# A float32 model block on one core: half of a step table on GpSimd, and query/key projections of the second attention carried as side products of the first

## The chip, the cores and the metric

The kernel runs on one core of a Trainium2 chip. The metric is device time in microseconds (us), lower is better. The kernel before took 3866.5 us, the median of three runs (3866.39 to 3875.27). All arithmetic is float32; a float32 matmul appears in the trace as two TensorE entries.

## The reference, cut to what matters

The model has a first block (two layers), then a second block of two layers, whose second layer is an attention mixer followed by a mixture of experts. Only the mixer is touched. From the normed hidden state `h` (512 tokens, width 1024) it computes:

```python
q_c, k_c, v_c, q_idx, k_idx, w_idx, q_d, k_d, v_d = split_cols_2(h @ w_in, CD_SIZES)
# first attention ("top-k"): 8 heads of 64; each query keeps the 128 keys with the best index score
score = relu(q_idx . k_idx), weighted by w_idx and summed over 8 index heads; causal
logit_c = q_c . k_c / 8 + bias_c[rel_bucket(dist)];  out_c = softmax(logit_c) @ v_c
# second attention ("diff"): 4 heads, two 64-wide halves each
b_d = rel_bias[:, 8:][rel_bucket(dist_d)]
attn = softmax(q1 . k1 / 8 + b_d) - lam * softmax(q2 . k2 / 8 + b_d);  out_d = attn @ v_d
```

`rel_bucket` maps a distance between positions to one of 32 buckets, and `rel_bias` holds one number for each bucket and each of the 12 heads. So a bias table of 12 heads x 512 queries x 512 keys is needed.

## The kernel before, in words

The kernel is a row of stages with a barrier of all engines between them; within a stage every engine runs its own program in a fixed order and waits on semaphores. The stages that matter here follow each other: `attn_front` (line 2267), the top-k attention, the diff attention (both `attention`, line 620), then `norm_and_out` (line 2492).

`attn_front` is one list of TensorE jobs (built in lines 2291 to 2364, run by `phase`, line 282). Each job writes one of eight PSUM banks in turn, and ScalarE moves it to SBUF. There are first the index projections and 32 index scores (line 2305), and six head projections q_c, k_c, v_c, q_d, k_d, v_d with four jobs each (one for 128 tokens: eight matmuls with 512 columns). Four scores follow each of the first six head jobs, and four bias jobs each of the next 16. The list is what sets the order on TensorE.

A bias job makes a part of the bias table. The 128 partitions hold four groups of 32 buckets, one for each quarter of a 128-query tile; `step[b, key] = 1` where the key is at most a bucket edge away from the query (line 2419, VectorE, one instruction with 512 columns for one query in each of the four quarters). The table of bias differences (128 x 48, block diagonal) times a step gives the bias of 12 heads for four queries. One bias job `g` (line 2322) does two steps, side by side in the array with output partitions 0 to 47 and 64 to 111. There are 64 jobs and three step buffers of two steps. ScalarE moves 112 rows to `out` (line 2338), and SyncE stores every second job's pair with two DMAs (line 2390) into a table in DRAM; ScalarE may reuse an `out` buffer when its store has landed.

VectorE, once the scores are summed, finds the best 128 keys: 16 rounds over four tiles, each a MAX8 (line 2449) and a MATCH_REPLACE8 (line 2450), and after each tile one pair of steps (`make_steps`, line 2414), which waits until the bias job that last used its buffer is done. The masks (lines 2455 and 2456) follow. GpSimd does nearly nothing in this stage.

`attention` runs 32 steps (head pair, query tile, head of the pair) of 128 queries x 512 keys. For each step: TensorE scores (line 754, in pairs), VectorE adds bias and finds the maximum (line 884), ScalarE takes the exponential (line 846), VectorE divides (line 903, or 908 for the difference), TensorE turns the probabilities (line 764), ScalarE moves them (line 829), TensorE weighs the values every four steps (line 782), VectorE stores (line 915). Before that queries and keys, which lie with tokens in the partitions, are turned on TensorE (line 741) and moved (lines 820 and 873). SyncE loads the bias from DRAM, and GpSimd adds the mask to it (line 687). With `side` an attention carries eight more projections: each is eight matmuls in its own bank, two after every step (`side_product`, line 718), its weights loaded by SyncE (line 711), its result moved by ScalarE (line 838). The four attentions of the first block do so; the two touched here do not.

Of the kernel before, what the change touches and what calls it, by code (L numbers as in the profile page):

```python
# [28 lines left out]
P = 128  # L29
# [9 lines left out]
HD = 64  # L39
# [580 lines left out]
def attention(chip, name, q, k, v, dk, out, gate=None, causal=True, scale=1.0, bias=None, masks=None, mix=None, decay=None,  # L620
              side=None, cleared_rows=None, scratch=None, early=None):
# [8 lines left out]
    fills = 2 if packed else 4  # L630
    with chip.stage(name) as st:
        n_turned = 2 * (1 if packed else 2)
        if scratch is None:
            turned_sb = [st.sb(f"turned{i}", [P, SEQ]) for i in range(2 * n_turned)]
        else:
            turned_sb = [part(scratch, i * SEQ, SEQ) for i in range(2 * n_turned)]
# [23 lines left out]
        def turned(which, m, a):  # L660

            return turned_sb[(m % 2) * n_turned + 2 * (0 if packed else a) + which]

        if bias is not None:
# [6 lines left out]
            def _(sp):  # L671
                for g in range(units):
# [26 lines left out]

        if side:  # L700
            side_w = [st.sb(f"side_w{i}", [P, DC, P]) for i in range(2)]
            side_loaded = [st.count(f"side_w{i}_loaded") for i in range(2)]
            side_summed, side_moved = st.count("side_summed"), st.count("side_moved")

            @st.block.sync
            def _(sp):
                for n, (w, _) in enumerate(side_jobs):
                    if n >= 2:

                        sp.wait_ge(*side_summed.at(n - 1))  # L710
                    sp.dma_start(side_w[n % 2][:, :, :], w.rearrange("(k p) n -> p k n", p=P)).then_inc(*side_loaded[n % 2].inc(16))
# [5 lines left out]
        def _(pe):  # L717
# [26 lines left out]
            def score(s):  # L744
                m, i, a = place(s)
                if i == 0:
# [65 lines left out]
        def _(act):  # L812
# [46 lines left out]
            for n in range(n_side):  # L859
                act.activation(side_jobs[n][1], side_jobs[n][1], ACT.Sigmoid)  # L860
# [1406 lines left out]
def attn_front(chip, io, fm, mod, scratch, topk, diff, causal, masks, ex, lambda_init):  # L2267
# [3 lines left out]
    Q4, M, N_SCORES, PAIRS = P // 4, 4 * BIAS_HEADS, TILES * IDX_HEADS, P // 2  # L2271
    STEPS, OUTS = 3, 2
    nq, nk = IDX_HEADS * IDX_DIM, IDX_DIM
    with chip.stage("attn_front") as st:
# [4 lines left out]
        steps_ = [st.sb(f"step{i}", [P, 2, SEQ]) for i in range(STEPS)]  # L2279
# [3 lines left out]
        cleared, pos_landed, table_landed = st.count("table_cleared"), st.count("positions_landed"), st.count("table_landed")  # L2283
# [75 lines left out]
        for n, job in enumerate(heads.jobs):  # L2359
# [3 lines left out]
            elif n < 22:  # L2363
                add_biases(4)
# [940 lines left out]
```

## Time and profile before

| | us |
|---|---|
| median of three runs | 3866.5 |
| the profiled execution | 3888.67 |
| its span in the profile | 3887.0 |
| TensorE busy in the span | 3343.7 (86%) |
| VectorE busy | 1586.1 (41%) |
| ScalarE busy | 722.0 (19%) |
| GpSimd busy | 194.9 (5%) |

The profile is of one execution. Its chain of waits that ended last reaches back only over the final stage, since the barriers cut it; so each stage is read by itself. In the views PE is TensorE, PEld its weight loads, DVE VectorE, ACT ScalarE, POOL GpSimd, SP SyncE; L12 is line 12 of the kernel. A matmul's end is modelled, so the time from one start to the next says more than its duration. PEclk is the granted TensorE clock as a share of full speed.

### The profile page before, as it was taken

The page shows a single profiled execution, that of the slowest core. Times are in us where ns is not written, and L with a number is a line of the kernel's source. Part 1 is how long each engine was busy: PE and PEld are TensorE (multiplying, and loading weights), DVE is VectorE, ACT ScalarE, POOL GpSimd, SP SyncE. Part 2 cuts the span into 40 slices and gives each one's busy share as a digit, 9 for nine tenths or more (in the row PEclk, how much of TensorE's full clock was granted, in tenths as well). Part 3 has the DMA queues.
Part 4 walks back from the last instruction along what each step waited for, and adds up shares of the span by engine and source line. Part 5 has one row for each costly group of instructions (what it writes and reads, how often), then busy time and mean ns, then how long its engine had stood idle before and what let it go on. Part 6 is the DMA issues. An engine that isn't in the chain of part 4 may idle for free. (4 is left out here: it accounts for less than half of the span.)

```text
span 3887.0 us, 42458 instructions
## 1 busy us (share of the span) xinstructions
PE 3343.7 (86%) x16176; PEld 1594.3 (41%) x16177; DVE 1586.1 (41%) x3043; ACT 722.0 (19%) x1428; POOL 194.9 (5%) x263
## 2 busy tenths in 40 slices
PE   8998997999899999799989767779599878688775
PEld 4454442774445443377334422223243344323221
DVE  3335556564314555766456400000248775100002
ACT  2132304111113321311001100000132353000001
POOL 0001010001000001000100000000100230000000
PEclk9999998999999999899999889999799999799997
DMA  2214461104211245100522589999433421999996
GB/s 95 83 38 172 149 215 41 29 8 149 96 44 49 65 141 160 32 20 7 197 87 83 237 368 428 428 428 361 131 118 120 102 66 53 385 427 423 429 428 276
DMA packets 208103, 696.55 MB, mean 179 GB/s; under 512 B 22248, under 2 KB 105704, under 8 KB 182736
## 3 DMA queue, kind: packets, MB, share of 16 engines
q1 hardware_dynamic: 178576, 589.42, 39.7%
q0 software_dynamic: 29376, 105.05, 7.4%
q8 instruction: 102, 1.67, 0.2%
q14 instruction: 49, 0.40, 0.0%
HBM read 636.14 MB, written 58.28 MB: 179 GB/s over the span
## 5 line engine op out<-in xcount | busy, mean ns | idle before, releaser
L348 PE MATMUL bank<-fm,w 128*128 128x512 f32 (+1 forms) x912 | 398.9, 598 | 14.2 <-DMA w<-in_ab_w_in 7.8
L2849 PE MATMUL bank<-experts_wu,experts_hs 128*64 128x512 f32 x1120 | 280.0, 658 | 73.6 <-DMA experts_wu<-in_moe_w_up 73.6
L348 PE MATMUL bank<-w,fm 128*128 128x512 f32 (+2 forms) x768 | 314.7, 566 | 6.2 <-DMA w<-in_w_in 6.2
L2849 PE MATMUL bank<-experts_wg,experts_hs 128*64 128x512 f32 x1120 | 267.4, 633 | 54.0 <-DMA experts_wg<-in_moe_w_gate 44.5
L2914 DVE TENSOR_TENSOR fm<-bank,fm 128x512 f32<-128x512 f32 x35 | 37.0, 1056 | 668.1 <-PE bank L2849 668.1
L2849 PE MATMUL bank<-experts_wd,fm 128*64 128x512 f32 x1120 | 254.8, 608 | 45.1 <-issue 22.9
L348 PEld LDWEIGHTS bank<-fm,w 128*128 128x128 f32 (+1 forms) x912 | 172.8, 190 | 237.7 <-issue 221.9
L729 PE MATMUL bank<-fm,side_w 128*128 128x512 f32 x512 | 249.4, 612 | 6.7 <-DMA side_w<-in_w_in 5.3
L348 PEld LDWEIGHTS bank<-w,fm 128*128 128x128 f32 x768 | 141.9, 195 | 178.5 <-issue 153.4
L2849 PEld LDWEIGHTS bank<-experts_wu,experts_hs 128*64 128x64 f32 x1120 | 86.4, 151 | 265.2 <-issue 170.5
L2849 PEld LDWEIGHTS bank<-experts_wg,experts_hs 128*64 128x64 f32 x1120 | 93.7, 145 | 223.8 <-issue 220.5
L2921 DVE TENSOR_TENSOR fm<-bank,mod 128x512 f32<-128x512 f32 x70 | 45.1, 686 | 326.4 <-PE bank L2849 326.4
L2849 PEld LDWEIGHTS bank<-experts_wd,fm 128*64 128x64 f32 x1120 | 82.9, 139 | 194.5 <-issue 166.0
L846 ACT ACTIVATE prob<-bank,nmax 128x128 f32<-128x128 f32 (+2 forms) x192 | 111.3, 580 | 210.8 <-DVE nmax L894 145.4
L729 PEld LDWEIGHTS bank<-fm,side_w 128*128 128x128 f32 x512 | 90.6, 196 | 88.8 <-issue 82.1
L2893 ACT ACTIVATE fm<-bank 128x512 f32<-128x512 f32 x35 | 20.9, 597 | 554.1 <-PE bank L2849 554.1
L1997 DVE SCALAR_TENSOR_TENSOR ada_sums<-ada_w,cond,ada_sums 128x1024 f32<-128x1024 f32 x84 | 105.8, 1282 | 37.4 <-DMA ada_w<-in_ada_w 36.5
L348 PE MATMUL bank<-w,merged 128*128 128x512 f32 x256 | 113.1, 600 | 3.1 <-DVE merged L1443 3.1
L2889 ACT ACTIVATE experts_hs<-bank 128x512 f32<-128x512 f32 x70 | 38.0, 595 | 409.1 <-PE bank L2841 409.1
L348 PE MATMUL bank<-o_fm,w 128*128 128x512 f32 x240 | 106.7, 604 | 6.5 <-DMA w<-in_w_pc 6.5
L764 PE MATMUL bank<-consts,prob 128*128 128x128 f32 x512 | 78.8, 282 | 29.1 <-ACT pT L829 11.5
L430 PE MATMUL bank<-fm,w 128*128 128x512 f32 x224 | 102.1, 610 | 1.6 <-ACT rwkv_a L1364 1.6
(492 smaller groups left out, 4618.6 us busy)
## 6 DMA issues: line engine op xcount, KB each, us to landing
experts_wg<-in_moe_w_gate SPq DMA_DIRECT2D x64, 2048.0 KB, 19.5
experts_wu<-in_moe_w_up SPq DMA_DIRECT2D x64, 2048.0 KB, 18.8
experts_wd<-in_moe_w_down SPq DMA_DIRECT2D x64, 2048.0 KB, 19.6
ada_w<-in_ada_w POOLq DMA_DIRECT2D x96, 512.0 KB, 4.9
expert_rows<-fm POOLq DMA_DIRECT2D x35, 512.0 KB, 10.4
fm<-expert_rows SPq DMA_DIRECT2D x33, 512.0 KB, 21.6
w<-in_w_in SPq DMA_DIRECT2D x16, 1024.0 KB, 5.5
side_w<-in_w_in SPq DMA_DIRECT2D x32, 512.0 KB, 4.0
```

Of the source, the lines that this page charges most:

```text
L348: ins = pe.matmul(bank, lhsT, rhs, start=(n == 0), stop=(n == len(todo) - 1))
L430: last = pe.matmul(out, lhsT, rhs, start=(n == 0), stop=(n == len(pairs) - 1))
L729: last = pe.matmul(SIDE[:, :], side_w[n % 2][:, k_, :], side_h[:, k_, :], start=(k_ == 0), stop=(k_ == DC - 1))
L764: last = pe.transpose(T[n % 2][:, j * P:(j + 1) * P], prob[s % 4][:, j * P:(j + 1) * P], chip.ident)
L846: act.activation(prob[s % 4][:, 0:n], S[s % n_scores][:, 0:n], ACT.Exp, bias=nmax[:, s:s + 1], scale=1.0 if bias is None else -1.0, accum_ ...
L1997: ins = dve.scalar_tensor_tensor(sums, self.slot[n % self.slots][:, :], by, sums, ALU.mult, ALU.add)
L2849: ins = pe.matmul(bank[rows, :], lhs[:, k, rows], weights[:, s, k, cols], start=(k == 0), stop=(k == chunks - 1))
L2889: ins = act.activation(hs[:, 4 * n:4 * n + 4, :], B[6 + n][:, :].rearrange("p (k n) -> p k n", k=4), ACT.Copy)
L2893: act.activation(act_out[:, :], B[0][:, :], ACT.Silu).then_inc(*silued.inc())
L2914: dve.tensor_tensor(dealt(hid[:, :], FC), B[1][:, :].rearrange("p (q k) -> p q k", k=FC), act_out[:, :].rearrange("p (q k) -> p q k", k=FC ...
L2921: ins = dve.tensor_tensor(y[:, cols], B[4 + d][:, :], gate_row[:, cols], ALU.mult)
```

## The change

Two things are changed.

First, the bias table. Steps are made in fours: VectorE makes two of each four, GpSimd the other two with the same instruction and a semaphore of its own. There are two buffers of four steps in place of three of two. A four has two bias jobs, one for each half of the partitions: job `half` takes 64 partitions of the four steps and of the table, and its four matmuls (64 partitions, 24 rows out) go to four column groups of the array, the other half's to the other 64 rows of the array and another bank. A four is stored by four DMAs in place of two. Seven bias jobs follow each head job from the seventh on, in place of four. VectorE makes its steps after every second tile in place of every tile.

Second, q_d and k_d (eight of the 24 head jobs) leave `attn_front`. The top-k attention carries them as eight side products, weights times `fm`, so that they come out with the head width in the partitions, as the diff attention wants them; the scale goes into ScalarE's move. The top-k attention then has three score banks in place of four. The diff attention gets them already turned, and does without its turning and its moves. Side weights are loaded by SyncE after the bias of the same number. The turned buffers of the top-k attention lie in the second half of `y`.

```diff
-    fills = 2 if packed else 4
+    fills = 0 if turned_in else 2 if packed else 4
...
-        if scratch is None:
+        if turned_in:
+            turned_sb = []
...
-            turned_sb = [part(scratch, i * SEQ, SEQ) for i in range(2 * n_turned)]
+            turned_sb = [part(scratch, scratch_at + i * SEQ, SEQ) for i in range(2 * n_turned)]
...
+            if turned_in:
+                return (q, k)[which][:, m, :]
...
+            def load_side(sp, n):
+                if n >= 2:
+
+                    sp.wait_ge(*side_summed.at(n - 1))
+                sp.dma_start(side_w[n % 2][:, :, :], side_jobs[n][0].rearrange("(k p) n -> p k n", p=P)
+                             ).then_inc(*side_loaded[n % 2].inc(16))
...
+                    if g < n_side:
+                        load_side(sp, g)
...
-                if i == 0:
+                if i == 0 and not turned_in:
...
-                    act.activation(side_jobs[n][1], SIDE[:, :], ACT.Copy).then_inc(*side_moved.inc())
+                    act.activation(side_jobs[n][1], SIDE[:, :], ACT.Copy, scale=side_scales[n] if side_scales else 1.0
+                                   ).then_inc(*side_moved.inc())
...
+    STEPS, OUTS = 2, 2
...
+        steps_ = [st.sb(f"step{i}", [P, 4, SEQ]) for i in range(STEPS)]
...
-        def bias(g):
-
-            b = g // 2
+        def bias(j):
+
+            f, half = divmod(j, 2)
+            rows, cols = slice(2 * Q4 * half, 2 * Q4 * (half + 1)), slice(TWO * half, TWO * (half + 1))
 
             def first(pe, moved):
-                pe.wait_ge(*stepped.at(g + 1))
+                if half == 0:
+                    pe.wait_ge(*stepped.at(f + 1))
+                    pe.wait_ge(*stepped_too.at(f + 1))
 
             def pairs(pe, bank):
-                for a in range(2):
-                    ins = pe.matmul(bank[64 * a:64 * a + M, :], table[:, :], steps_[g % STEPS][:, a, :], start=True, stop=True,
-                                    tile_position=(0, 64 * a))
+                for a in range(4):
+                    ins = pe.matmul(bank[Q4 * a:Q4 * a + TWO, :], table[rows, cols], steps_[f % STEPS][rows, a, :], start=True, stop=True,
+                                    tile_position=(2 * Q4 * half, Q4 * a))
                 return ins
 
             def ahead(act, moved):
-                if g % 2 == 0 and b >= OUTS:
-                    act.wait_ge(*stored[b % OUTS].at(32 * (b // OUTS)))
+                if half == 0 and f >= OUTS:
+                    act.wait_ge(*stored[f % OUTS].at(4 * 16 * (f // OUTS)))
             return Job(None, pairs, lambda bank: bank[:, :], "act", lambda act, ps: act.activation(
-                outs[b % OUTS][0:64 + M, g % 2, :], ps[0:64 + M, :], ACT.Copy), first, ahead)
+                outs[f % OUTS][0:P - Q4 + TWO, half, :], ps[0:P - Q4 + TWO, :], ACT.Copy), first, ahead)
...
-        for names, dsts in ((("q_c", "k_c", "v_c"), topk), (("q_d", "k_d", "v_d"), diff)):
+        for names, dsts in ((("q_c", "k_c", "v_c"), topk), (("v_d",), (diff_v,))):
...
             if n < 6:
                 add_scores(4)
-            elif n < 22:
-                add_biases(4)
-        dst = scratch.rearrange("a t n k -> a (t n) k")
+            else:
+                add_biases(min(7, 2 * FOURS - len(biased_at)))
+        dst = scratch.rearrange("(q r) t n k -> r q (t n) k", q=2)
...
-            while 2 * begun[0] + 1 < PAIRS and biased_at[2 * begun[0] + 1] < upto:
-                b = begun[0]
-                sp.wait_ge(*moved(biased_at[2 * b + 1]))
-                for a in range(2):
-                    sp.dma_start(dst[:, 4 * b + a:4 * b + 4:2, :], outs[b % OUTS][64 * a:64 * a + M, :, :]).then_inc(*stored[b % OUTS].inc(16))
+            while begun[0] < FOURS and biased_at[2 * begun[0] + 1] < upto:
+                f = begun[0]
+                sp.wait_ge(*moved(biased_at[2 * f + 1]))
+                for a in range(4):
+                    sp.dma_start(dst[:, :, 4 * f + a, :], outs[f % OUTS][Q4 * a:Q4 * a + TWO, :, :]).then_inc(*stored[f % OUTS].inc(16))
                 begun[0] += 1
...
+            pool.wait_ge(*quartered.at(1))
+            for f in range(FOURS):
+                if f >= STEPS:
+                    pool.wait_ge(*done(biased_at[2 * (f - STEPS) + 1]))
+                for a in (2, 3):
+                    at = at_quarter + 4 * f + a
+                    ins = pool.tensor_scalar(steps_[f % STEPS][:, a, :], pos[:, 0:SEQ], pos[:, at:at + 1], None, ALU.is_le)
+                ins.then_inc(*stepped_too.inc())
...
-            def make_steps(g):
-                if g >= STEPS:
-                    dve.wait_ge(*done(biased_at[g - STEPS]))
+            def make_steps(f):
+                if f >= STEPS:
+                    dve.wait_ge(*done(biased_at[2 * (f - STEPS) + 1]))
                 for a in range(2):
-                    at = at_quarter + 2 * g + a
-                    ins = dve.tensor_scalar(steps_[g % STEPS][:, a, :], pos[:, 0:SEQ], pos[:, at:at + 1], None, ALU.is_le)
+                    at = at_quarter + 4 * f + a
+                    ins = dve.tensor_scalar(steps_[f % STEPS][:, a, :], pos[:, 0:SEQ], pos[:, at:at + 1], None, ALU.is_le)
                 ins.then_inc(*stepped.inc())
...
-                        g += 1
+                    if t % 2 and f < FOURS:
+                        make_steps(f)
+                        f += 1
...
                 attention(chip, "topk_attention", q, k, lambda h, j: v[:, j, h, :], HD, y_fm, causal=False,
-                          scale=HD ** -0.5, bias=bias_of, masks=masks)
+                          scale=HD ** -0.5, bias=bias_of, masks=masks,
+                          side=(fm, [(io["cd_w_in"][0][:, CD[name] + c * P:CD[name] + (c + 1) * P], dst[:, c, :])
+                                     for name, dst in (("q_d", diff_q), ("k_d", diff_k)) for c in range(DIFF_HEADS)]),
+                          scratch=y_fm, scratch_at=DIFF_HEADS * SEQ, side_scales=[HD ** -0.5] * DIFF_HEADS + [1.0] * DIFF_HEADS)
...
-            attention(chip, "diff_attention", q, k, lambda m, j: vd[:, j, m, :], HD, mixed, causal=False, scale=HD ** -0.5,
+            vd = diff_v[:, :, :, :].rearrange("p t (h a) d -> p t h (a d)", a=2)
+            attention(chip, "diff_attention", diff_q, diff_k, lambda m, j: vd[:, j, m, :], HD, mixed, causal=False, turned_in=True,
```

## Rows read from the trace of the kernel before

**Rows 1.** Stretches: bounds, width, busy PE, PEld, DVE, ACT, POOL, then PEclk, DMA share, GB/s.
```profile
3070.60:3152.10 81.50, 61.06 (x352) 32.51 (x352) 58.03 (x140) 42.36 (x100) 38.57 (x16) 0.92 0.43 104
...
3152.10:3223.00 70.90, 52.33 (x224) 28.52 (x224) 58.94 (x156) 34.78 (x84) 18.90 (x8) 0.95 0.23 60
2886.50:3056.60 170.10, 170.10 (x513) 62.83 (x512) 141.94 (x317) 47.79 (x80) 0.00 (x0) 1.00 0.36 111
```

**Rows 2.** Timeline, TensorE in attn_front: start, us, engine, line, operation, operands, count.
```profile
2954.30 3.64 PE L2331 MATMUL bank<-step,table 128*48 128x512 f32 x16
2957.87 7.13 PE L348 MATMUL bank<-w,fm 128*128 128x512 f32 x16
...
3053.59 14.00 PE L348 MATMUL bank<-w,fm 128*128 128x512 f32 x32
```

**Rows 3.** Timeline, VectorE in attn_front; in brackets the idle time before, with its releaser.
```profile
2887.42 0.69 DVE L2449 MAX8 best<-attn_masks 128x8 f32<-128x512 f32 x1
...
2955.84 0.88 DVE L2419 TENSOR_SCALAR step<-pos 128x512 f32<-128x512 f32 x2 [1.78 <-PE bank L2331]
2956.64 0.69 DVE L2449 MAX8 best<-attn_masks 128x8 f32<-128x512 f32 x1
...
3053.51 0.69 DVE L2449 MAX8 best<-attn_masks 128x8 f32<-128x512 f32 x1
...
3056.55 0.43 DVE L2455 TENSOR_SCALAR attn_masks<-attn_masks 128x512 f32<-128x512 f32 x1
...
3060.57 0.69 DVE L2456 TENSOR_TENSOR attn_masks<-attn_masks,attn_causal 128x512 f32<-128x512 f32 x1
```

**Rows 4.** Two pairs of score matmuls on different row halves of the array, timeline.
```profile
3110.97 1.13 PE L754 MATMUL bank<-turned 64*128 64x512 f32 x4
```

**Rows 5.** GpSimd's groups of instructions: busy us, mean ns, then idle time before.
```profile
L687 POOL TENSOR_TENSOR bias<-bias,attn_masks 128x1024 f32<-128x1024 f32 x16 | 38.6, 2425 | 297.0 <-DMA bias<-bias_scratch 296.9
...
L694 POOL MEMSET zero<- 128x1024 f32 x1 | 1.0, 951 | 356.4 <-POOLq L120 356.4
```

**Rows 6.** Timeline of the top-k attention: VectorE's division beside GpSimd's mask additions, and alone.
```profile
3107.71 4.83 POOL L687 TENSOR_TENSOR bias<-bias,attn_masks 128x1024 f32<-128x1024 f32 x2 [0.62 <-DMA bias<-bias_scratch]
...
3108.09 2.24 DVE L903 TENSOR_SCALAR prob<-prob,sums 128x512 f32<-128x512 f32 x1
...
3113.88 0.49 DVE L903 TENSOR_SCALAR prob<-prob,sums 128x512 f32<-128x512 f32 x1
```

**Rows 7.** Lines 2338 and 2390: count, ns min/median/max, first and last start; landing time.
```profile
L2338 ACT ACTIVATE out<-bank x64: 597/597/600, 2891.6 to 3053.7; 112x512 f32<-112x512 f32 x64
...
L2390 SPq DMA_DIRECT2D bias_scratch<-out x64: 302/384/687, 2893.1 to 3054.7; - x64
...
DMA to landing us min/median/max: 2.4/2.8/6.5
```

**Rows 8.** Timeline, TensorE in the top-k attention around a long wait.
```profile
3092.87 1.12 PE L764 MATMUL bank<-consts,prob 128*128 128x128 f32 x4 [2.48 <-DVE prob L903]
3093.91 2.08 PE L754 MATMUL bank<-turned 64*128 64x512 f32 x4
```

**Rows 9.** Timeline, TensorE in an attention of the first block that carries eight side products.
```profile
1316.16 0.63 PE L741 MATMUL bank<-consts,fox_q 128*128 128x128 f32 x4 [1.05 <-PEq L120]
...
1321.07 5.30 PE L729 MATMUL bank<-fm,side_w 128*128 128x512 f32 x8
...
1414.12 1.74 PE L782 MATMUL bank<-pT,fox_v 128*64 128x256 f32 x16 [0.69 <-ACT pT L829]
```

**Rows 10.** Timeline, SyncE at the start of the top-k attention: bias loads.
```profile
3070.69 11.11 SPq L678 DMA_DIRECT2D bias<-bias_scratch  x24
```

**Rows 11.** DMA issues on the page: out<-in, engine, count, KB each, us to landing.
```profile
side_w<-in_w_in SPq DMA_DIRECT2D x32, 512.0 KB, 4.0
```

**Rows 12.** VectorE's moves of turned keys in the diff attention: busy us, mean ns.
```profile
L873 DVE COPY turned<-bank 128x512 f32<-128x512 f32 x4 | 2.7, 683 | 2.3 <-PE bank L741 2.3
```

More of the change, by code:

```diff
@@ L620, in attention @@
 def attention(chip, name, q, k, v, dk, out, gate=None, causal=True, scale=1.0, bias=None, masks=None, mix=None, decay=None,
-              side=None, cleared_rows=None, scratch=None, early=None):
+              side=None, side_scales=None, turned_in=False, cleared_rows=None, scratch=None, scratch_at=0, early=None):
     steps, pairs = HEADS * TILES, HEADS // 2
@@ L660, in turned, with _ @@
         def turned(which, m, a):
+            if turned_in:
+                return (q, k)[which][:, m, :]
             return turned_sb[(m % 2) * n_turned + 2 * (0 if packed else a) + which]
+        if side:
+            side_w = [st.sb(f"side_w{i}", [P, DC, P]) for i in range(2)]
+            side_loaded = [st.count(f"side_w{i}_loaded") for i in range(2)]
+            side_summed, side_moved = st.count("side_summed"), st.count("side_moved")
+            def load_side(sp, n):
[3 more added lines that the diff above has]
+                             ).then_inc(*side_loaded[n % 2].inc(16))
+            if bias is None:
+                @st.block.sync
+                def _(sp):
+                    for n in range(n_side):
+                        load_side(sp, n)
         if bias is not None:
@@ L698, in _ @@
                 pool.wait_ge(*wiped.at(wiped.total))
[L700 to L711, printed above, removed]
         if early is not None:
@@ L858, in _ @@
                 act.wait_ge(*side_moved.at(n_side))
-            for n in range(n_side):
+            for n in range(n_side if side_scales is None else 0):
                 act.activation(side_jobs[n][1], side_jobs[n][1], ACT.Sigmoid)
@@ L2264, in conv_mixers, with attn_front @@
         routed.programs()
-def attn_front(chip, io, fm, mod, scratch, topk, diff, causal, masks, ex, lambda_init):
+def attn_front(chip, io, fm, mod, scratch, topk, diff_v, causal, masks, ex, lambda_init):
     w_in = io["cd_w_in"][0]
-    Q4, M, N_SCORES, PAIRS = P // 4, 4 * BIAS_HEADS, TILES * IDX_HEADS, P // 2
-    STEPS, OUTS = 3, 2
+    Q4, N_SCORES, M = P // 4, TILES * IDX_HEADS, 4 * BIAS_HEADS
+    FOURS, TWO = P // 4, 2 * BIAS_HEADS
+    STEPS, OUTS = 2, 2
     nq, nk = IDX_HEADS * IDX_DIM, IDX_DIM
@@ L2278, in attn_front @@
         lam, pr = st.sb("lam", [P, 4, HD]), st.sb("pr", [P, 2, HD])
-        steps_ = [st.sb(f"step{i}", [P, 2, SEQ]) for i in range(STEPS)]
+        steps_ = [st.sb(f"step{i}", [P, 4, SEQ]) for i in range(STEPS)]
         outs = [st.sb(f"out{i}", [P, 2, SEQ]) for i in range(OUTS)]
@@ L2432, in _ @@
             link(dve.tensor_tensor(table[:, :], table[:, :], before[:, :], ALU.subtract))
-            for g in range(STEPS):
-                make_steps(g)
+            for f in range(STEPS):
+                make_steps(f)
             for n in range(N_SCORES):
@@ L2444, in _ @@
                 dve.wait_ge(*added.at(n + 1))
-            g = STEPS
+            f = STEPS
             for _ in range(TOPK // 8):
@@ L2473, in attn_mixers @@
         with ExitStack() as diff_heads:
-            diff = [sb(f"diff_{n}", [P, TILES, 2 * DIFF_HEADS, HD], diff_heads, side="right") for n in "qkv"]
+            diff_q, diff_k = (sb(f"diff_{n}", [P, DIFF_HEADS, SEQ], diff_heads, side="right") for n in "qk")
+            diff_v = sb("diff_v", [P, TILES, 2 * DIFF_HEADS, HD], diff_heads, side="right")
             with ExitStack() as topk_heads:
                 topk = [sb(f"topk_{n}", [P, TILES, HEADS, HD], topk_heads, side="right") for n in "qkv"]
-                attn_front(chip, io, fm, mod, scratch, topk, diff, causal, masks, ex, lambda_init)
+                attn_front(chip, io, fm, mod, scratch, topk, diff_v, causal, masks, ex, lambda_init)
                 y_fm = sb("y", [P, DC, SEQ])
```

10 lines of the change are left out of this document (5 added, 5 removed).

## The prediction, made before the changed kernel was run

> **What bounds the kernel now.** The chain that ended last covers only the last stage, so I read the touched stages one by one: first the stretches table, then each engine's timeline inside a stage, then the waits. In attn_front TensorE is busy 170.1 of 170.1 us while VectorE is at 141.9 [rows 1], and VectorE's steps wait for it [rows 3]: TensorE sets the end, VectorE is 16% behind. In the top-k attention (3070.6 to 3152.1, 81.5 us) TensorE is busy 61.1 and VectorE 58.0; in the diff attention (70.9 us) VectorE 58.9 and TensorE 52.3 [rows 1]. So the change takes TensorE work from a stage where it is the bound and puts it where some 20 us of TensorE are idle. What matters is who is next in the first and how far the second grows.
>
> **The front without eight head jobs.** A head job takes 14.0/2 = 7.0 us (3.64 of bias behind it start to start 7.1); I use 7.06, so 8 x 7.06 = 56.5 us leave TensorE [rows 2]. Four bias jobs take 2957.87 - 2954.30 = 3.57 us, 0.89 each, with two column groups side by side [rows 2]. A four is eight matmuls on two row halves and four column groups. Two score pairs on different row halves run together: four entries in 1.13 us, some 0.54 for each of two passes [rows 4]. Eight at once appears nowhere. Bounds for a four are 1.07 (all together, as in [rows 4]) and 2 x 0.89 = 1.79 (halves one after the other); I take 1.07, since both kinds of sharing show. From the start of the seventh head job TensorE then has 10 x 7.06 + 32 x 1.07 = 105 us, where it had 184.
>
> **VectorE is next.** Two tiles of the search without steps take 3056.55 - 3053.51 = 3.04 us, and two steps 2956.64 - 2955.84 = 0.80 [rows 3]. The search has 32 such pairs of tiles, and 30 fours are made within it: 32 x 3.04 + 30 x 0.80 = 121.3 us from 2887.42, so 3008.7; the masks, 3056.55 to 3061.3, add 4.7 [rows 3]. Nothing can end the stage before 3013.4: of the 56.5 + 23 us taken from TensorE at most 55 can come back.
>
> **GpSimd's steps.** No such instruction is in the trace. Lower bound: half a memset of 1024 columns, 0.48 us; upper: half of a two-input addition of 1024 columns, whose mean is 2.43, so 1.21 [rows 5]. One input lies between; I take 0.9, 1.8 a four, under VectorE's 3.84. The price that counts is another: a VectorE division that takes 0.49 us alone took 2.24 beside GpSimd's addition and ended just after its end [rows 6]. The Trainium skill (SBUF — State Buffer, SBUF: two separate sides) says that the pair of ports is locked for a whole instruction and the loser blocks; by that rule moving a step from VectorE to GpSimd can cost VectorE a wait as long as the step, which speaks against this change. What saves it is time: GpSimd starts four f+2 when TensorE is done with f, 1.1 us after VectorE made f, and is through at 2.9, while VectorE is in its 3.04 of search. They meet only when both waited for the same buffer; there I charge 1.0 us. The Trainium skill (GPSIMD Engine Reference, 3.1 Elementwise — side-by-side cycle accounting) has 769 ns for 512 elements in its best case; that would take 0.3 off two such waits and leave the sum.
>
> **The cycle, by hand.** Seven fours go with two head jobs. Let H be the start of a head job, with the last four just half done. VectorE makes the next four at H+3.3, comes to the one after at H+6.4 and waits: its buffer is the half-done one. TensorE ends the head job at 7.1, the half at 8.0, and VectorE, with GpSimd in its way, is done at 9.8 (GpSimd at 10.2). The next is made at 13.6, TensorE done 14.7, second head job to 21.8; meanwhile fours are made at 17.5 and 21.3, then 25.2 and 29.0, and at H+29.9 it starts over. That is 3.0 more than 7 x 3.84. TensorE idles 2.5 to 2.8 us at a time in it. The trace shows what such a wait does: after 2.48 us idle the four turns took 1.12 us and the two score pairs behind them 2.08 [rows 8] for 1.13 [rows 4], the granted clock being at its lower level, 1.2 GHz for 2.4. At half speed for some 3.4 us a head job takes 1.7 more; the one before the blocked buffer passes it on. Period 31.6 us with this, 29.9 without.
>
> The first group has two fours ready; the search waits at 2890.5, and the next head job starts at about 2898.3. Four periods later, at 3024.7 (3017.9 without the clock), all but half a four is done. Then come the last head job 7.06 (+1.7), the last half four 0.9, ScalarE's move 0.6, four stores at 0.38 and a landing of 2.8 [rows 7], 0.5 of barrier: 3039.8, or 3031.3. I take 3037: 33.6, say 34 us earlier than 3070.6. ScalarE and SyncE keep up: two moves, four issues and a landing are 5.5 us, less than the 7.7 in which an out buffer comes round. SyncE's wait for stores holds only the v_d weights back, which have four groups of slack.
>
> **The top-k attention with side products.** An attention of the first block has the same arrangement: eight side products, two matmuls a step, three score banks. It ran from 1316.16 to 1415.86, 99.7 us [rows 9], with causal widths, 5/8 of these on average. Of the 61.1 us here [rows 1] some 5 are turns of q and k and a few the lower clock, so 3/8 of about 50, 19 us, is the most that full widths add; with the fixed part of each matmul 16 (13 to 19). There the first side product starts 4.9 us after the stage [rows 9]; here its weights are issued behind eight bias loads at 0.46 us each [rows 10] and take 4.0 to land [rows 11], so 8.3: +3.4, with nothing behind it on TensorE going ahead, as it works in order. Sum 99.7 + 16 + 3.4 = 119.1, which is +37.6. The other way: 61.1 + 56.5 = 117.6, plus 5 of start and less 3 of clock, 119.6. VectorE's 58 and ScalarE's 42 + 5 us are well under it, and the contention of [rows 6] is now hidden. The side weights wait on SyncE for a side product two before; the bias behind them has eight steps of slack.
>
> **The diff attention.** Its start is set by bias, mask and first maximum, so the early turns save nothing. Of four moves three lie in the body where VectorE is the bound: 3 x 0.68 [rows 12] = 2 us. Between 0 and 4.
>
> **Sum.** -34 + 37.5 - 2 = +1.5 us, on 3888.7 profiled. The profiled execution is 22 us above the median of 3866.5; the difference is put on the median: 3868.
>
> **Rivals.** (1) Faster. The clock stays up in the front's waits (3031.3, -39.3), the widths add 13 and the side weights come in the shadow of the turns (+31.7), diff -4: -11.6, with cheap GpSimd steps -14: 3853. For it: TensorE is in a head job half of the time. Against: waits of 2.5 us. (2) The two row halves do not overlap, so a four takes 1.79. Three fours in a period see it, about 2.5 us, x4, and the tail: +11, 3879. Against it stands [rows 4]. (3) Slower, one mechanism: the GpSimd step. From 1.92 us each (2 x 1.92 = 3.84) GpSimd sets the pace and VectorE meets its lock every time. At 2.43, as much as the addition of twice the columns, VectorE waits some 2.4 us in each of 30 fours, 72 less the 12 it loses now anyway: 60 on top of the sum, 3928. (4) The move does nothing for VectorE: lock waits as long as the saved steps in every four, +0.9 x 30 less 12 = +15: 3883; it needs GpSimd to fall in step with VectorE. The rule of the Trainium skill (SBUF — State Buffer, SBUF: two separate sides) is this rival if the two always meet; [rows 6] bears out the lock, not the meeting.
>
> **How the numbers follow.** Forecast 0.49 (own range 3857 to 3879), rival 1 0.27, rival 2 0.12, rival 3 0.04, rival 4 0.08. Range 3849 to 3886: it leaves out rival 3 and the ends of 1 and 4. About 0.3%, 11.6 us, is what a measurement here tells from no change. Faster 0.28, same 0.48, slower 0.24: rivals 2, 3 and 4 are slower, the forecast counts as same.
>
> **What would show it.** Right: VectorE's search without gaps but one a pair of head jobs, its steps 0.4 to 0.5 us but after those gaps; eight L2331 entries starting within 0.1 us; attn_front 34 us shorter, TensorE under 75% in it; the top-k attention at 119 with TensorE over 93%; the diff attention's start unchanged. Wrong: step instructions on VectorE of over 1 us throughout (rival 4), GpSimd busy without a break (3), a four of 1.8 us (2), granted clock 1.00 in the front (1). A top-k attention under 112 or over 125 us would break the term it rests on most.

## The result, and the profile after

The changed kernel takes 3904.9 us (median of 4 runs, 3900.8 to 3910.7), the kernel before, beside it, 3870.9 (3866.4 to 3877.7): a ratio of 1.0086 [1.0066, 1.0107], 33 us more (26 to 41). I had predicted 3868 with a range up to 3886. The time is 19 us above the end of the range, and slower than before.

The profiled execution of the changed kernel has 3905.1 us and a span of 3903.4. The profiled one of the kernel before has 3888.7, 18 us above its own median, so the two profiles differ by 16 us only; they are compared here stage by stage. First the stretches that answer to [rows 1]: attn_front from the first maximum of the search, the top-k attention, the diff attention. Columns: bounds, width, busy PE, PEld, DVE, ACT, POOL (instructions), granted clock, DMA share, GB/s.

```profile
2875.80:3054.40 178.60, 132.28 (x664) 41.91 (x662) 132.76 (x263) 41.77 (x76) 100.56 (x60) 0.78 0.30 83
3054.40:3173.80 119.40, 113.23 (x480) 54.96 (x480) 54.31 (x140) 47.43 (x108) 37.90 (x16) 0.94 0.45 106
3173.80:3245.00 71.20, 52.02 (x192) 28.80 (x192) 55.84 (x152) 32.68 (x80) 18.86 (x8) 0.86 0.22 60
```

The same three stretches of the kernel before are 183.2, 81.5 and 70.9 us (the first is cut here from the first maximum, 2887.4, to the stage's end, 3070.6; its row):

```profile
2887.40:3070.60 183.20, 180.19 (x536) 67.00 (x534) 145.82 (x324) 50.47 (x84) 0.00 (x0) 1.00 0.34 104
```

So the front is 4.6 us shorter where I had 34, the top-k attention 37.9 longer where I had 37.6, and the diff attention unchanged where I had 2 less. The three together are 33.6 us longer, as much as the medians differ. All other stages, which are the same code, are 17 us shorter in this profile than in the one of before. (11.6 of these lie ahead of the first maximum, and the front's first conversion of positions comes as much earlier.)

The front is where the account failed. Before, TensorE was busy all the time at clock 1.00. Now it is busy 132 of 179 us at 0.78, VectorE 133, GpSimd 101: none of the three is full. That is the sign of a cycle in which they wait for one another. TensorE's timeline shows it (start, us, engine, line, operation; in brackets the idle time before it and its releaser), beside [rows 2]:

```profile
2936.16 1.91 PE L2348 MATMUL bank<-step,table 64*24 64x512 f32 x24
2940.87 1.28 PE L2348 MATMUL bank<-step,table 64*24 64x512 f32 x16 [2.79 <-POOL step L2427]
2944.33 1.95 PE L2348 MATMUL bank<-step,table 64*24 64x512 f32 x16 [2.18 <-POOL step L2427]
2946.21 8.23 PE L348 MATMUL bank<-w,fm 128*128 128x512 f32 x16
2954.38 1.94 PE L2348 MATMUL bank<-step,table 64*24 64x512 f32 x32
2959.18 1.95 PE L2348 MATMUL bank<-step,table 64*24 64x512 f32 x16 [2.86 <-POOL step L2427]
2962.64 1.92 PE L2348 MATMUL bank<-step,table 64*24 64x512 f32 x8 [1.51 <-POOL step L2427]
```

Three things stand in it. A four is sixteen entries (eight matmuls, two passes). Two fours with all data at hand take 1.94 us (the x32 group), 0.97 each: the row halves do overlap. TensorE idles 1.5 to 2.9 us again and again, and here always for a step of GpSimd. And the head job behind such waits takes 8.23, the next one from 2964.48 9.33, for 7.13 before: every head job of the front runs partly at the lower clock. From 2908.52 to 2946.21, seven fours and two head jobs, it is 37.7 us; the mean period is 37.6. I had 31.6.

VectorE's side of the same period, to be read against [rows 3], and GpSimd's:

```profile
2937.36 1.23 DVE L2444 TENSOR_SCALAR step<-pos 128x512 f32<-128x512 f32 x2 [6.71 <-PE bank L2348]
...
2941.53 1.23 DVE L2444 TENSOR_SCALAR step<-pos 128x512 f32<-128x512 f32 x2
...
2955.66 1.23 DVE L2444 TENSOR_SCALAR step<-pos 128x512 f32<-128x512 f32 x2 [1.49 <-PE bank L2348]
```

```profile
2937.34 13.25 POOL L2427 TENSOR_SCALAR step<-pos 128x512 f32<-128x512 f32 x8 [9.14 <-PE bank L2348]
2955.65 10.18 POOL L2427 TENSOR_SCALAR step<-pos 128x512 f32<-128x512 f32 x6 [5.06 <-PE bank L2348]
```

VectorE's pair of steps takes 1.23 us or more nearly every time, not only behind a wait: GpSimd, once released, works 13 us without a break and so nearly always runs beside it (56 of VectorE's 64 steps). The pace of VectorE without waits is 2941.53 - 2937.36 = 4.17 us a four where I had 3.84. And once in a period it waits 6.7 us for the buffer of a four whose second half TensorE does only behind the head job.

The price of a GpSimd step is the number that the trace of before did not have (count, ns min/median/max, first and last start). In the stretch ahead of the search, with VectorE idle but for its first moments, and then in the search:

```profile
L2427 POOL TENSOR_SCALAR step<-pos x4: 1550/1553/1658, 2797.5 to 2802.2; 128x512 f32<-128x512 f32 x4
```

```profile
L2427 POOL TENSOR_SCALAR step<-pos x60: 1554/1720/1844, 2880.2 to 3035.9; 128x512 f32<-128x512 f32 x60
```

1.55 us alone, where my bounds were 0.48 and 1.21. The 1.72 is the median of two kinds: 25 of the 64 steps, with VectorE idle or in its search, have a median of 1.56, and the 39 that overlap a step of VectorE 1.78. One of each, and the pair of VectorE's steps that meets the second:

```profile
2939.17 1.56 POOL L2427 TENSOR_SCALAR step<-pos 128x512 f32<-128x512 f32 x1
2940.70 1.78 POOL L2427 TENSOR_SCALAR step<-pos 128x512 f32<-128x512 f32 x1
2941.53 0.49 DVE L2444 TENSOR_SCALAR step<-pos 128x512 f32<-128x512 f32 x1
2941.93 0.83 DVE L2444 TENSOR_SCALAR step<-pos 128x512 f32<-128x512 f32 x1
```

VectorE's first step begins and ends, at its usual 0.49 us, while GpSimd's step from 2940.70 to 2942.48 is still running; only the second is longer, by 0.34. The two slow each other when their steps meet, but neither keeps the other out for a whole step.

The waits of the whole front (engine and line, what it waited for: us in total, times, longest):

```profile
PE bank L2348 <- POOL step L2427: 41.8, 18, 2.9
DVE step L2444 <- PE bank L2348: 34.2, 9, 6.8
```

The 41.8 and 34.2 us lie partly beside each other, so they are not a sum. Which of the causes (the price, the shared port, the blocked buffer, the clock) carries how much, the trace does not say; the experiments do.

### The profile page after: what moved, and what is told of

Read it like the earlier page. It is cut to its first block and busy times, and to the rows that moved or that the text cites. A ratio compares the mean times of both kernels' runs of the same rounds, so it can differ in the third digit from the quotient of the medians.

```text
span 3903.4 us, 42897 instructions
## 1 busy us (share of the span) xinstructions
PE 3351.6 (86%) x16400; PEld 1588.3 (41%) x16401; DVE 1564.8 (40%) x2975; ACT 715.9 (18%) x1424; POOL 301.3 (8%) x327
## 5 line engine op out<-in xcount | busy, mean ns | idle before, releaser
L348 PE MATMUL bank<-fm,w 128*128 128x512 f32 (+1 forms) x912 | 399.5, 599 | 12.7 <-DMA w<-in_ab_w_in 7.6
L740 PE MATMUL bank<-fm,side_w 128*128 128x512 f32 x640 | 314.3, 616 | 8.5 <-DMA side_w<-in_w_in 5.5
L348 PE MATMUL bank<-w,fm 128*128 128x512 f32 (+2 forms) x640 | 273.0, 585 | 6.3 <-DMA w<-in_w_in 6.3
L348 PEld LDWEIGHTS bank<-w,fm 128*128 128x128 f32 x640 | 123.7, 205 | 162.6 <-issue 150.6
L740 PEld LDWEIGHTS bank<-fm,side_w 128*128 128x128 f32 x640 | 113.7, 197 | 116.8 <-issue 107.8
L2427 POOL TENSOR_SCALAR step<-pos 128x512 f32<-128x512 f32 x64 | 106.8, 1684 | 146.6 <-PE bank L2348 133.3
```

Of the source, the lines that this page charges most:

```text
L348: ins = pe.matmul(bank, lhsT, rhs, start=(n == 0), stop=(n == len(todo) - 1))
L740: last = pe.matmul(SIDE[:, :], side_w[n % 2][:, k_, :], side_h[:, k_, :], start=(k_ == 0), stop=(k_ == DC - 1))
L2427: ins = pool.tensor_scalar(steps_[f % STEPS][:, a, :], pos[:, 0:SEQ], pos[:, at:at + 1], None, ALU.is_le)
```

## The experiments

The theory before the first four was that the two halves of the change each do what their stages show, and that GpSimd's price sets the front. In the table, "front" is from the first maximum to the end of attn_front (the first bias load of the next stage), "period" seven fours with two head jobs, all from the profiles; the ratio is against the kernel before on the same chip.

| kernel | ratio [95%] | front us | period us | head jobs us |
|---|---|---|---|---|
| before | 1 | 183.2 | | 7.1 |
| after | 1.0086 [1.0066, 1.0107] | 178.6 | 37.6 | 8.2 to 9.5 |
| side_only | 1.0059 [1.0034, 1.0084] | 170.5 | | 7.1 to 9.3 |
| table_gpsimd_only | 0.9923 [0.9902, 0.9945] | 156.1 | | 7.1 |
| table_vector_only | 0.9921 [0.9898, 0.9944] | 158.3 | | 7.1 |
| all_steps_on_vector | 1.0073 [1.0048, 1.0098] | 175.9 | 37.3 | 8.1 to 9.6 |
| whole_fours | 1.0017 [0.9999, 1.0034] | 146.8 | 30.7 | 7.1, 7.7 |
| whole_fours_vector | 1.0023 [1.0010, 1.0035] | 153.4 | 32.4 | 7.1 to 9.1 |
| half_steps | 1.0043 [1.0025, 1.0061] | 161.4 | 34.2 | 8.8 to 9.3 |
| half_columns | 1.0029 [1.0016, 1.0042] | 162.2 | 34.3 | 8.7 to 9.1 |
| four_buffers | 0.9975 [0.9956, 0.9995] | 137.0 | 29.4 | 7.1 to 9.4 |
| four_buffers_whole | 0.9978 [0.9965, 0.9992] | 136.9 | 29.4 | 7.1 to 9.2 |

**side_only**: the bias table of before, with the side products of the change.

```diff
-                for a in range(4):
-                    ins = pe.matmul(bank[Q4 * a:Q4 * a + TWO, :], table[rows, cols], steps_[f % STEPS][rows, a, :], start=True, stop=True,
-                                    tile_position=(2 * Q4 * half, Q4 * a))
+                for a in range(2):
+                    ins = pe.matmul(bank[64 * a:64 * a + M, :], table[:, :], steps_[g % STEPS][:, a, :], start=True, stop=True,
+                                    tile_position=(0, 64 * a))
```

> The bias table stays as in the kernel before (pairs of steps, three buffers, VectorE alone, two column groups); only the query and key projections of the diff attention move to side products, and the 64 bias jobs are dealt seven to each of the last ten head jobs. Theory A (the front is paced by whoever makes the steps, and GpSimd's 1.7 us step is what took the gain): VectorE needs 64 x 1.52 + 61 x 0.80 + 4.7 = 151 us from its first MAX8, plus some 5 of waits and a tail of 13 (head job, last bias, store), so the front ends about 20 us earlier than before; the top-k attention 119 us (+38): total +17 us. Rival B (the side products cost 38 us and the front cannot give anything back whatever makes the steps): +34 us, as with the whole change.

It is 23 us slower (13 to 33), between the two expectations. The front is 12.7 us shorter, the top-k attention 118.6 us. Moving eight head jobs out of the front buys 13 us there and costs 37 in the attention.

**table_gpsimd_only** and **table_vector_only**: the change's table without the side products, once with GpSimd's half and once with all four steps on VectorE.

```diff
-        for names, dsts in ((("q_c", "k_c", "v_c"), topk), (("v_d",), (diff_v,))):
+        for names, dsts in ((("q_c", "k_c", "v_c"), topk), (("q_d", "k_d", "v_d"), diff)):
-                add_biases(min(7, 2 * FOURS - len(biased_at)))
+                add_biases(min(4, 2 * FOURS - len(biased_at)))
```

and table_vector_only besides, with GpSimd's loop left out:

```diff
-                for a in range(2):
+                for a in range(4):
```

> Only the bias table is changed (fours, two row halves, half of the steps on GpSimd); the projections stay in the front as 24 head jobs, and four bias jobs follow each head job from the seventh on. Theory A: two fours a head job need 2 x 3.44 = 6.9 us of GpSimd, which fit into the 7.1 us of the head job and 2.0 us of bias; TensorE keeps the front with 16 x 9.2 + 14.1 us and it ends some 20 us earlier than before; both attentions as before: total -20 us. Rival B (GpSimd's steps and the port lock cost wherever they stand): the front no shorter than before, total 0 to +15 us.

> As the run with the bias table alone, but VectorE makes all four steps of each four (no GpSimd). Theory A: VectorE's 32 x 3.04 + 30 x 1.60 + 4.7 = 150 us fit under TensorE's 161, so this too ends the front some 20 us earlier: total -20 us, within 5 us of the run with GpSimd. Rival B: 15 us or more faster than the run with GpSimd.

Both are 30 us faster than before, the best of all kernels here; I had expected 20. The front of the first:

```profile
2934.95 1.94 PE L2348 MATMUL bank<-step,table 64*24 64x512 f32 x32
2936.82 7.13 PE L348 MATMUL bank<-w,fm 128*128 128x512 f32 x16
2943.88 1.94 PE L2348 MATMUL bank<-step,table 64*24 64x512 f32 x32
2945.75 7.13 PE L348 MATMUL bank<-w,fm 128*128 128x512 f32 x16
```

TensorE never waits, the clock stays up, and the bias behind a head job costs 1.87 us start to start (2945.75 - 2943.88) where 3.57 stood in [rows 2]. GpSimd's step costs 1.72 us here as well, and it does not matter:

```profile
L2427 POOL TENSOR_SCALAR step<-pos x64: 1552/1722/1847, 2789.8 to 3003.9; 128x512 f32<-128x512 f32 x64
```

As long as TensorE is the bound, neither GpSimd's price nor who makes the steps shows in the ratios. (The front of the second is 2.2 us longer: from 2952.58 on its head jobs start every 9.24 us for 8.94, which is two of VectorE's 4.6 us a four with four steps in each.) The two halves of the change alone give -30 and +23, and together +33, not -7: some 40 us are lost by their meeting (each of the three is known to 8 or 10 us).

**all_steps_on_vector**: the whole change, but GpSimd makes nothing.

```diff
-            pool.wait_ge(*quartered.at(1))
-            for f in range(FOURS):
...
-                ins.then_inc(*stepped_too.inc())
...
-                for a in range(2):
+                for a in range(4):
```

> The whole change, but VectorE makes all four steps. Theory A: the blocked four costs 1.6 us of VectorE in place of 3.4 of GpSimd, the period of seven fours falls from 37.6 to about 34.9 us, the front is 12 us shorter than with the whole change: +22 us against before. Rival B (not GpSimd but the two buffers, the seven bias jobs in a row and the clock set the front): no shorter than with the whole change, +34 us or more, since VectorE has 24 us more to do.

This fell out against the theory that GpSimd's price sets the front: the front is 2.7 us shorter than the changed kernel's, not 12, with GpSimd away altogether. The ratio, +28 us (19 to 38), lies between the two expectations and does not decide. VectorE now makes four steps in 1.67 us, and waits once a period:

```profile
2963.49 1.67 DVE L2435 TENSOR_SCALAR step<-pos 128x512 f32<-128x512 f32 x4
...
2973.05 1.67 DVE L2435 TENSOR_SCALAR step<-pos 128x512 f32<-128x512 f32 x4 [4.98 <-PE bank L2347]
2977.66 1.67 DVE L2435 TENSOR_SCALAR step<-pos 128x512 f32<-128x512 f32 x4
```

Its pace is 4.61, and 7 x 4.61 + 4.98 = 37.3 is the period. So the second theory: seven bias jobs behind a head job are three fours and a half. The half-done four keeps one of the two step buffers through a whole head job, whoever makes the steps. The runs that follow test this from several sides.

**whole_fours** and **whole_fours_vector**: eight and six bias jobs by turns, so that no four is split.

```diff
-                add_biases(min(7, 2 * FOURS - len(biased_at)))
+                add_biases(min(6 if n % 2 else 8, 2 * FOURS - len(biased_at)))
```

> After, with eight and six bias jobs by turns behind the head jobs instead of seven each, so that no four is half done when a head job runs. Theory A (a half-done four holds one of the two step buffers through a whole head job, and the waits that this makes are the 8 us a period that are missing): seven fours and two head jobs take 29.5 to 32 us instead of 37.6, the front is some 20 to 30 us shorter than the changed kernel's 178.6, and the whole 4 to 14 us longer than before. Theory B (GpSimd's 1.72 us a step and the port that it shares with VectorE set the front, however the jobs are grouped): the period stays above 36 us, the front within 6 us of 178.6, the whole 28 to 36 us longer than before.

> All steps on VectorE, none on GpSimd, and eight and six bias jobs by turns. Theory A (the blocked buffer): the one wait of 4.98 us that all_steps_on_vector had in each period goes, the period is VectorE's own 4.61 x 7 = 32.3 us instead of 37.3, the front some 20 us shorter than that kernel's 175.9, and the whole 6 to 14 us longer than before. Theory B (the grouping is beside the point): front within 5 us of 175.9, the whole 22 to 34 us longer than before.

Both came as the blocked buffer has it: fronts 31.8 and 22.5 us shorter than with sevens, periods 30.7 and 32.4. The waits of whole_fours:

```profile
DVE step L2444 <- PE bank L2348: 6.5, 9, 1.4
...
PE bank L2348 <- POOL step L2427: 33.3, 14, 2.9
```

VectorE's waits fall from 34.2 to 6.5 us, though TensorE still waits 33 for GpSimd, and the head jobs are back at 7.1 and 7.7:

```profile
2925.54 1.09 PE L2348 MATMUL bank<-step,table 64*24 64x512 f32 x16 [2.87 <-POOL step L2427]
2926.55 7.13 PE L348 MATMUL bank<-w,fm 128*128 128x512 f32 x16
```

The grouping alone is worth some 27 us (1.0086 against 1.0017). Between these two, GpSimd's half is worth 6.6 us of front; the ratios do not part them.

**half_steps** and **half_columns** take GpSimd's price away and leave the sevens. In the first GpSimd makes nothing and TensorE reads VectorE's two steps twice (half of the queries get a wrong bias); in the second GpSimd writes 256 of its 512 columns (half of the keys in half of the queries).

```diff
-                    ins = pe.matmul(bank[Q4 * a:Q4 * a + TWO, :], table[rows, cols], steps_[f % STEPS][rows, a, :], start=True, stop=True,
+                    ins = pe.matmul(bank[Q4 * a:Q4 * a + TWO, :], table[rows, cols], steps_[f % STEPS][rows, a % 2, :], start=True, stop=True,
```

```diff
-                    ins = pool.tensor_scalar(steps_[f % STEPS][:, a, :], pos[:, 0:SEQ], pos[:, at:at + 1], None, ALU.is_le)
+                    ins = pool.tensor_scalar(steps_[f % STEPS][:, a, 0:SEQ // 2], pos[:, 0:SEQ // 2], pos[:, at:at + 1], None, ALU.is_le)
```

> After without GpSimd's half of the steps: VectorE makes the first two of each four and TensorE reads them in the place of the other two as well, so the bias table is wrong for half of the queries. The grouping in sevens stays. It is the changed kernel with GpSimd's steps at no price and no shared port: VectorE's pace falls to 3.04 + 0.80 = 3.84 us a four, which is what the prediction reckoned with. Theory A (the blocked buffer alone makes the waits): one wait a period stays, 3.84 x 7 + 5 to 8 = 32 to 35 us, and the front is 13 to 25 us shorter than 178.6; the whole 9 to 21 us longer than before. Theory B (GpSimd's price made the waits): the period is 28.5 to 31 us, as the prediction had it, the front 28 to 36 us shorter, and the whole within 8 us of before.

> After with GpSimd writing only the first 256 of the 512 columns of each of its steps; the other 256 are zeroed once, so half of the bias table is wrong. Sevens and two buffers stay. Theory A (GpSimd's price is by the column and by VectorE's use of the port): a step takes 0.78 to 0.95 us, which is the 0.9 that the prediction took, a pair of VectorE's steps 1.0 to 1.25 us, the period 34.5 to 36.5 us, between the 34.2 of half_steps and the 37.6 of the changed kernel, and the front 163 to 173 us; the whole 17 to 28 us longer than before. Theory B (a fixed price for each instruction of GpSimd): a step stays above 1.3 us, and the period at 37 to 38 us. If the front falls to 150 us or less, the account of the clock is wrong.

```profile
L2429 POOL TENSOR_SCALAR step<-pos x64: 910/921/1284, 2796.6 to 3021.3; 128x256 f32<-128x256 f32 x64
```

half_columns happens to give a step the very price that I had put in, 0.92 us, so it is close to the kernel that my sum described. Its period is 34.3 (a hair under what I expected of it) and not 31.6, with every head job slowed:

```profile
2904.15 1.95 PE L2348 MATMUL bank<-step,table 64*24 64x512 f32 x16 [1.92 <-DVE step L2446]
2906.02 8.83 PE L348 MATMUL bank<-w,fm 128*128 128x512 f32 x16
2914.79 1.94 PE L2348 MATMUL bank<-step,table 64*24 64x512 f32 x32
2918.39 1.09 PE L2348 MATMUL bank<-step,table 64*24 64x512 f32 x16 [1.66 <-POOL step L2429]
2921.39 1.92 PE L2348 MATMUL bank<-step,table 64*24 64x512 f32 x8 [1.92 <-DVE step L2446]
2923.24 8.76 PE L348 MATMUL bank<-w,fm 128*128 128x512 f32 x16
```

The whole is 11 us longer than before (6 to 16), less than the 17 to 28 that I had expected of it, though the three stages in its profile are 17 us longer (352.8 for 335.6). half_steps, 17 us longer than before as expected (10 to 24), has VectorE at my 3.84 a four and its one long wait, beside one of 1.9 in each period:

```profile
2919.73 0.88 DVE L2435 TENSOR_SCALAR step<-pos 128x512 f32<-128x512 f32 x2 [5.62 <-PE bank L2347]
...
2923.56 0.88 DVE L2435 TENSOR_SCALAR step<-pos 128x512 f32<-128x512 f32 x2
...
2927.38 0.88 DVE L2435 TENSOR_SCALAR step<-pos 128x512 f32<-128x512 f32 x2
```

GpSimd for nothing, or at 0.92 us a step, is the same front (161.4, 162.2). So a price of 0.9 is indeed hidden; one of 1.72 is not: 178.6 - 162.2 = 16.4 us.

**four_buffers** and **four_buffers_whole**: the third and fourth step buffer lie in diff_q and diff_k, which the top-k attention fills only later; the second has the eight and six by turns too.

```diff
-    STEPS, OUTS = 2, 2
+    STEPS, OUTS = 4, 2
-        steps_ = [st.sb(f"step{i}", [P, 4, SEQ]) for i in range(STEPS)]
+        steps_ = [st.sb(f"step{i}", [P, 4, SEQ]) for i in range(2)] + [diff_q, diff_k]
```

> After with four step buffers instead of two (the third and fourth lie in the memory of the turned queries and keys of the second attention, which is free until the front is over); sevens stay and GpSimd still makes half. Theory A (too few buffers for a head job of 7 to 9 us): VectorE's waits for TensorE go, VectorE paces the loop at 4.18 us a four with two fours more made ahead, 32 x 3.04 + 28 x 1.23 = 132 us from the first maximum to the end of the loop, the front 147 to 155 us instead of 178.6, and the whole from 2 us less to 10 us more than before. Theory B (GpSimd's steps at 3.44 us a four are late whenever TensorE asks): TensorE still waits for GpSimd, the front 165 to 178 us, the whole 20 us or more longer than before.

> Four step buffers and eight and six bias jobs by turns, together. Theory A (four_buffers already leaves VectorE with next to no waits, so VectorE's own 132 us are the floor of the loop): the front is within 4 us of the 137.0 of four_buffers, and the whole 4 to 14 us less than before. Theory B (each cure takes its own part of the 42 us): the front is 128 us or less, the whole 18 us or more less than before.

137.0 us of front, and VectorE is at last the bound (130.5 busy of 137.0):

```profile
2879.30:3016.30 137.00, 111.96 (x664) 39.09 (x662) 130.48 (x258) 41.89 (x76) 92.20 (x56) 0.89 0.39 108
```

It is 10 us less than the least that I had expected: the search ends after 131.4 us (at 3010.7), as reckoned with 132, but then TensorE has nothing left to catch up with, and the stage ends 5.6 us later and not 15. The grouping adds nothing to it (136.9): with four buffers a half-done four blocks nobody, and 137 is VectorE's floor. That is the change made as well as I know how, and it is 10 us faster than before (2 to 17), against 30 for the table alone. The reason can be read off the fronts. The table alone ends at 156.1, and VectorE's floor is 137: taking eight head jobs away buys at most 19 us, and the top-k attention grows by 37 for it.

## Why the prediction was wrong, step by step

- **"TensorE sets the end, VectorE is 16% behind", "VectorE is next"**: right. With four buffers the front ends at VectorE's own work.
- **A four at 1.07 us**: right; 1.09 alone (half of one alone takes 1.06), 1.94 for two in a row. Rival 2 is out.
- **"The top-k attention 119.1"**: right, 119.4 with TensorE busy 95%. Its first side product starts 3063.13 - 3054.44 = 8.7 us into the stage (8.3 said), 3.8 later than in the stage that I had built on; that leaves 119.4 - 99.7 - 3.8 = 15.9 for the wider rows, where I had 16. So both terms are right, each for itself:

```profile
3063.13 4.64 PE L740 MATMUL bank<-fm,side_w 128*128 128x512 f32 x5 [1.68 <-DMA side_w<-in_cd_w_in]
```

- **"GpSimd's steps ... I take 0.9"**: the step that failed first. 1.55 us alone, 1.72 in the median of the front. The upper bound was half of a two-input addition of 1024 columns, 1.21 [rows 5]; I had reasoned that one input must be cheaper than two. By the undisturbed steps of half_columns a column costs (1550 - 910)/256 = 2.5 ns and an instruction 0.27 us on top. So half of an instruction is no bound for an instruction of half the width: the part on top does not halve. If it is the same for the addition, which no run shows, 512 columns of it would take 0.27 + (2.43 - 0.27)/2 = 1.35 us (an estimate), and the comparison against a column of scalars is dearer than that too. The Trainium skill (GPSIMD Engine Reference, 3.1 Elementwise — side-by-side cycle accounting) gives 769 ns for 512 elements at best, the nearest figure to one input; the trace has twice that. The price of the steps is worth 16.4 us of the 29 missing (178.6 against half_columns' 162.2).
- **"They meet only when both waited for the same buffer; there I charge 1.0 us"**: wrong in how often. GpSimd at 3.44 us a four has no gap before VectorE's next pair; the pair takes 1.23 instead of 0.88 us in nearly every four, 0.35 x 7 = 2.4 us a period. The Trainium skill (SBUF — State Buffer, SBUF: two separate sides) has an exclusive hold for a whole instruction. The trace does not agree for these steps: one of VectorE's runs from 2941.53 to 2942.02 at its usual 0.49 us in the middle of one of GpSimd's (2940.70 to 2942.48), 26 of the 64 lie wholly inside one, and the wait "as long as the step" never came; it was 0.35 us a pair, a fifth of GpSimd's step. This was what rival 4 had (VectorE pays in every four) at some 40% of its price, 0.35 for 0.9, and rival 3's condition (1.92 us) nearly met: it took both. I had given them 0.12 together and priced each as if the other did not happen.
- **"At half speed for some 3.4 us a head job takes 1.7 more", on one of two head jobs**: right on the mechanism and on the size (8.7 to 9.1 us in half_columns for 7.1), wrong on the count. In half_columns both head jobs of a period are slowed, and the bias jobs before each take 1.95 us for 1.09. The second head job alone adds 1.7 and the bias jobs 1.7 more, part of it beside waits that were there anyway: 34.3 us a period for my 31.6. The clock is not all of these 2.7 us: VectorE comes to the blocked buffer 4.8 us after the head job's start (3.8 in the changed kernel), not 6.4, and waits there for 5.1. How much of it is the clock's and how much that of the hand cycle's order, no run shows. The front of half_columns is 162.2 where my sum has 183.2 - 34 = 149.2: 13 us. Four periods make 11 of it. 3 more come from my own rounding: the hand cycle ended at 3039.8 and I took 3037, without a reason; some 1 us goes the other way. 13 + 16.4 = 29 is what is missing from -34.
- **The hand cycle** had the half-done four and VectorE's wait for it, and gave 31.6 us. What I did not do was ask what the cycle would be without it. With whole fours 31.8 us of front go, both terms above together: they are not prices that must be paid but what the blocked buffer makes of them, since VectorE's 4.18 us a four are more than GpSimd's 3.44. (A slip beside it: from 3070.6 to 3013.4, the least end that I had worked out, are 57 us and not 55; nothing hangs on it.)
- **The diff attention, -2**: all four moves are gone (VectorE has 152 instructions for 156, and is busy 55.8 us for 58.9 [rows 1]) and the stage is as long as before. From its start to the first maximum are 7.2 us in both, as I said. The saved work turned into idle time; the granted clock there is 0.86 for 0.95 before, and whether that took the gain was not tried.
- **Chances**: slower by over 0.3% had 0.24. The profile had what was needed to give it more: a sum of +1.5 made of -34 and +37.5, of which the second was bounded closely by a stage of the same kind, and the first rested on a price that no row showed and a cycle of three engines with two buffers. In that cycle a clock that stayed up gave 6 us (3037 to 3031.3), while every price that I had too low made a wait in each period. The range should have reached further up than down; it was laid evenly round the sum.

## What to carry to other kernels

When work is taken from the bound of a stage, look first at how far the next engine is below it: here 19 us were to be had for 37 paid, and that alone decided against the move. When two or three engines hand buffers round, count the buffers against the longest job that can come between two halves of one hand-over; a group size that is no multiple of the unit cost 27 us, and two more buffers in memory that was free took that cost away. A price that the trace does not show is safely bounded only by the same operation at the same width; the bound from half of another one failed here.

## What the runs showed of the chip

- GpSimd's comparison of 512 columns with a column of scalars takes 1.55 us alone and 1.56 beside VectorE's search, and 1.78 where it overlaps VectorE's steps; of 256 columns 0.92. VectorE does 512 in 0.49.
- Beside it, two such steps of VectorE take 1.23 us for 0.88. A whole one of them, 0.49 us, can run while GpSimd's is under way.
- Eight matmuls of 64 rows by 24 columns, on two row halves and four column groups, take 1.09 us together and 0.97 in a row of them; the four of one row half alone take 1.06.
- Waits of 1.5 to 2.9 us between short jobs can put the granted clock to its lower level (1.2 GHz for 2.4) for the job behind them: 8.2 to 9.5 us in the changed kernel for head jobs of 7.1. They need not: with one wait of 2.87 us in whole_fours the head job takes 7.1, with one of 2.74 in half_steps 9.2. Waits of 0.9 to 1.2 us, three ahead of each head job, did not in side_only once the job had run at 7.1 (its first ones took 7.7 to 9.3):

```profile
2966.31 1.07 PE L2343 MATMUL bank<-step,table 128*48 128x512 f32 x4 [1.24 <-DVE step L2431]
2968.62 1.07 PE L2343 MATMUL bank<-step,table 128*48 128x512 f32 x4 [1.24 <-DVE step L2431]
2969.61 7.13 PE L348 MATMUL bank<-w,fm 128*128 128x512 f32 x16
```
